# A two-layer decoder trunk on eight cores: the fused stage's turn reordered, decays and gate folded into weights and constants, and loads moved

## The reference

```python
mod = silu(c) @ w_mod[layer] + b_mod[layer]      # 6 rows of 1024
shift_m, scale_m, gate_m, shift_f, scale_f, gate_f = split(mod, 6)
h = rms_norm(x, norm_mix[layer]) * (1 + scale_m) + shift_m
x = x + gate_m * token_mixer(h, ...)
h = rms_norm(x, norm_ffn[layer]) * (1 + scale_f) + shift_f
x = x + gate_f * (swiglu(h) if layer == 0 else moe_swiglu(h))   # top 2 of 8 experts
```

## Time and profile before

| | us |
|---|---|
| median of 3 runs | 4345.12 |
| lowest and highest | 4304.47, 4496.92 |
| the profiled execution | 4326.1 |
| its span, slowest core (1) | 4324.4 |
| spans of the cores | 4235.2 to 4324.4 |
| PE busy | 3081.8 (71%) |
| DVE, ACT, POOL busy | 1214.9, 1066.3, 581.2 |

### The profile page before, as it was taken

The page is one execution under the profiler, slowest core; times in us unless marked ns, Lnnn a source line. Parts: engine busy times, 40 slices in busy tenths (PEclk is TensorE's granted clock), DMA queues, the critical chain, the costliest instruction groups (busy, mean ns, idle before and its releaser), DMA issues.

```text
span 4324.4 us, 48809 instructions; the slowest of 8 cores (4235.2 to 4324.4 us)
## 1 busy us (share of the span) xinstructions
PE 3081.8 (71%) x16488; PEld 1538.1 (36%) x16497; DVE 1214.9 (28%) x1896; ACT 1066.3 (25%) x1873; POOL 581.2 (13%) x644
## 2 busy tenths in 40 slices
PE   2266666676569998788666543999966597768776
PEld 1112222233224444233333222645433254435433
DVE  2223334355512314133443332212111111112111
ACT  2223333333211111355332221212121112112111
POOL 1100000022200101000022221011121121202120
PEclk7566565577789999788677776999988799989998
DMA  5442342301284333313111128649596969698884
GB/s 145 95 116 79 101 116 86 98 25 49 97 122 74 93 59 84 75 24 58 66 39 37 49 64 153 105 70 166 79 164 110 177 102 151 99 150 124 120 132 68
DMA packets 311799, 412.93 MB, mean 95 GB/s; under 512 B 62604, under 2 KB 225956, under 8 KB 311469
## 3 DMA queue, kind: packets, MB, share of 16 engines
q0 software_dynamic: 219056, 257.81, 39.8%
q1 hardware_dynamic: 92414, 150.83, 11.1%
HBM read 577.17 MB, written 59.06 MB: 147 GB/s over the span
## 4 chain that ended last, share of the span: by engine, by line
PE 56%; DMA 17%; DVE 10%; ACT 7%; issue 6%; POOL 1%; SPq 1%; DVEq 0%; ACTq 0%; POOLq 0%; PEldq 0%
PE ps L1430 13%; PE ps L1458 10%; PE ps L1072 7%; DMA t_w2m<-moe_w 5%; DMA t_ring<-moe_w 4%; PE ps L1003 4%; PE ps L1104 4%; PE ps L789 3%; PE ps L754 3%; PE ps L718 3%; DMA t_bm<-b_mod 2%; DMA ebrep<-ebscr 2%; DVE t_mev L613 2%; PE ps L907 2%; DMA t_w<-ffn_w 1%
## 5 line engine op out<-in xcount | busy, mean ns | idle before, releaser
L1430 PE MATMUL ps<-t_hgT,t_ring 128*128 128x0 bf16 (+1 forms) x5376 | 840.0, 318 | 213.1 <-DMA t_ring<-moe_w 109.9
L1430 PEld LDWEIGHTS ps<-t_hgT,t_ring 128*128 128x128 bf16 x5376 | 523.6, 100 | 530.1 <-issue 276.4
L1458 PE MATMUL ps<-t_w2m,t_gTm 128*128 128x512 bf16 x1960 | 434.4, 385 | 81.7 <-DMA t_w2m<-moe_w 80.9
L1434 DVE TENSOR_TENSOR t_gTm<-ps,t_sam 128x384 bf16<-128x384 f32 (+1 forms) x336 | 217.3, 647 | 837.8 <-ACT t_sam L1433 830.6
L1072 PE MATMUL ps<-hT,t_w 128*128 128x512 bf16 x1408 | 311.7, 385 | 41.5 <-DMA t_w<-ffn_w 40.2
L1458 PEld LDWEIGHTS ps<-t_w2m,t_gTm 128*128 128x128 bf16 x1960 | 193.5, 99 | 320.1 <-issue 96.5
L1433 ACT ACTIVATE t_sam<-ps 128x384 bf16<-128x384 f32 (+1 forms) x336 | 187.2, 562 | 473.4 <-PE ps L1430 448.6
L1433 ACT ACT_TABLE_LOAD x56 | 71.8, 1283 | 773.1 <-PE ps L1430 773.1
L754 PE MATMUL ps<-t_qT,t_kT 64*128 64x256 bf16 (+1 forms) x768 | 210.2, 388 | 56.0 <-ACT t_pr L758 50.0
L766 DVE TENSOR_TENSOR t_pr<-t_pr,t_EB 128x512 bf16<-128x512 bf16 (+1 forms) x320 | 127.9, 406 | 415.6 <-ACT t_pr L758 412.4
L907 PE MATMUL ps<-t_wr,hT 128*128 128x512 bf16 x768 | 193.5, 414 | 44.2 <-DVE t_wr L888 44.2
(11 more groups left out here) (241 smaller groups left out, 3090.5 us busy)
## 6 DMA issues: line engine op xcount, KB each, us to landing
t_ring<-moe_w POOLq DMA_DIRECT2D x112, 1024.0 KB, 27.1
t_w2m<-moe_w POOLq DMA_DIRECT2D x56, 1024.0 KB, 38.4
t_wm<-w_mod SPq DMA_DIRECT2D x40, 1024.0 KB, 5.4
t_w<-ffn_w POOLq DMA_DIRECT2D x20, 1024.0 KB, 9.3
t_wmi<-w_mod SPq DMA_DIRECT2D x8, 1024.0 KB, 16.5
t_n0x<-x SPq DMA_DIRECT2D x16, 512.0 KB, 11.3
t_n1x<-x SPq DMA_DIRECT2D x16, 512.0 KB, 3.6
xs<-t_n1x SPq DMA_DIRECT2D x16, 512.0 KB, 2.7
```

Source lines behind the costliest of these rows:

```text
L1430: ins = e.matmul(o, lhsT=ring[:, s_, kc, j * 128:(j + 1) * 128], rhs=r, start=(kc == 0), stop=(kc == 7))
L1434: k.op("dve", lambda e: e.tensor_tensor(out=gT[:, fc, c0:c0 + width], in0=ps[:, bb, 0:width], in1=sa[z][:, 0:width], op=ALU.mult), reads=[ ...
L1458: ins = e.matmul(ps[:, b0 + hf, :], lhsT=gT[:, fc, b * 128:(b + 1) * 128], rhs=w2s[:, fc, hf * 512:(hf + 1) * 512], start=(fc == 0), stop= ...
```

## The change

Constants: the decay of q is no longer multiplied in. It is common to a token's retention output, which the norm per head divides out; only the term 128 EPS under the root is divided by the decay's square (c_dec, added by POOL at L1024 of the new file). The decay of k goes onto v in ACT's copy (four of 128 columns, each with its own scale). The gate of the mixer, gate_m, and the gain ret_gain go into wo (`gated_wo`, on DVE, from fp32 pieces of w_out that SP loads). So the gate product, POOL's product with gB and one DVE pass of the rotary step go.

Order: `eb_rows` stands behind the norm's loop. `proj` alternates between two pairs of banks for the first pair of heads. pv runs three batches behind scores. 12 of the 20 modulation items stay in layer 0, 8 go to layer 1, at fixed batches; all bias rows are loaded once, and DVE adds them. wr, wst, the centring and wo are loaded and worked inside attention. In the fused stage a turn begins with `project`, `evacuate` and `outproj`, and statistics come last. `ffn_open` loads the first two groups of w1 and w3 in turn 16 of layer 0's fused stage, and each group of w2 is loaded one group ahead. Buffers move to make room.

```diff
-    c["c_dec"] = np.concatenate([qdec, kdec], axis=1).astype(np.float32)
+    c["c_dec"] = np.concatenate([128.0 * EPS / qdec ** 2, kdec], axis=1).astype(np.float32)
...
         def residual(self, t, halves, tmpo=None, Btmpo=None):
...
-                for hf, bank in enumerate(halves):
+                for hf, bank in halves:
                     c = slice(512 * hf, 512 * hf + 512)
-                    k.op("dve", lambda e: e.tensor_tensor(out=tmpo[:, c], in0=ps[:, bank, :], in1=gate2[:, g, c], op=ALU.mult),
-                         reads=[PB[bank], GB[g]], writes=[Btmpo])
-            k.op("dve", lambda e: e.tensor_tensor(out=xt, in0=xt, in1=tmpo, op=ALU.add), reads=[Btmpo, Bxt], writes=[Bxt])
+                    k.op("dve", lambda e: e.tensor_tensor(out=xt[:, c], in0=ps[:, bank, :], in1=xt[:, c], op=ALU.add), reads=[PB[bank], Bxt], writes=[Bxt])
...
+    def eb_rows():
         k.dma("sp", bass.AP(ebscr, 0, [[384, 8], [8 * 384, 3], [1, 384]]), ebst[:], reads=[Beb], writes=[ebscr_buf])
-        for i_ in range(24):
+        for i_ in [8 * b_ + h for h in range(8) for b_ in range(3)]:
...
-        k.dma("sp", bm[:], bmod_d[l:l + 1, nb * 512:(nb + 1) * 512], writes=[Bbm])
...
+        k.op("pe", lambda e: e.matmul(ps[0:32, bank, :], lhsT=onesq[:], rhs=mev[:], start=True, stop=True), reads=[Bmev, B["const"]], writes=[PB[bank]])
+        n = len(mod_q)
+        k.op("dve", lambda e: e.tensor_tensor(out=mrow[0:n, :], in0=ps[0:n, bank, :], in1=bm[:], op=ALU.add), reads=[PB[bank], Bbm], writes=[Bmrow])
...
-        for tb in range(4):
-            for j in range(2):
-                r_ = proj(0, j, tb)
-                r_()
+        prev = None
+        for n, (tb, j) in enumerate((tb, j) for tb in range(4) for j in range(2)):
+            rest = proj(0, j, tb, 6 - 2 * (n % 2), 7 - 2 * (n % 2))
+            if prev is not None:
+                prev()
+            prev = rest
+        prev()
...
+        LAG = 3
+        mod_open(12 if l == 0 else 8)
...
-                    if l == 0 and i < 18:
-                        if i % 6 == 2:
-                            mod_half(0)
-                        elif i % 6 == 4:
-                            mod_half(1)
-                        elif i % 6 == 5:
-                            mod_end(7)
+                    if i in (3, 11):
+                        mod_half(0)
+                    elif i in (6, 14):
+                        mod_half(1)
+                    elif i in (8, 16):
+                        mod_end(7)
+                    if (c, hh, i) in late:
+                        late[(c, hh, i)]()
...
+        attention(l, attnT, BattnT, {(1, 0, 1): load_wr, (3, 0, 1): load_late, (3, 0, 9): centre, (3, 1, 1): open_wo, (3, 1, 9): half_wo})
...
+            for h in range(4):
+                c = slice(128 * h, 128 * h + 128)
+                k.op("act", lambda e: e.activation(out=rv[:, t % 5, c], in_=ps[:, 1, c], func=AF.Copy, scale=dec[:, 4 + h:5 + h]), reads=[PB[1], B["oh"]], writes=[Brv[t % 5]])
+            k.op("act", lambda e: e.activation(out=sgg[:, t % 5, :], in_=ps[:, 2, :], func=AF.Silu), reads=[PB[2]], writes=[Bsgg[t % 5]])
...
         for i in range(NT + 9):
+            at(i, 0, project)
+            at(i, 0, evacuate)
+            at(i, 6, outproj)
+            at(i, 4, gated)
+            at(i, 6, lambda t: n2.residual(t, ((1, 4), (0, 7))))
+            at(i, 7, norm_a)
             at(i, 1, turn_qk)
-            at(i, 1, state)
             at(i, 2, inner)
-            at(i, 4, gated)
             at(i, 3, outer)
             at(i, 5, turn_ret)
-            at(i, 6, outproj)
...
+            at(i, 1, state)
             at(i, 8, norm_b)
+            at(i, 6, n2.stats)
...
+    def ffn_open():
+        F["w13"] = P("w13", [128, 2, 2, 8, 512], BF16, 157, n=2)
+        ffn_load13(0)
+        ffn_load13(1)
...
+                if gi + 1 < n:
+                    load2(gi + 1)
```

More of the change, by code:

```diff
@@ L646, in build, with attention @@
         BVg[z_].lo, BVg[z_].hi = vv0 + 24 * KB + 12 * KB * z_, vv0 + 36 * KB + 12 * KB * z_
-    def attention(l, mixT, BmixT):
+    def attention(l, mixT, BmixT, late):
         qT, BqT = P("qT", [128, 2, S], BF16, 48, n=2)
@@ L823, in attention @@
                 pend = None
-                for i in range(nb_ + 2):
+                for i in range(nb_ + LAG):
                     if i < nb_:
@@ L998, in outproj @@
         def outproj(t):
[L999 removed]
+            for hf, bk in ((1, 4), (0, 7)):
                 def mm(e):
@@ L1077, in up @@
                          reads=[PB[bb], Bsa[i2]], writes=[BgT])
-        load13(0)
-        load13(1)
-        for gi in range(n):
-            load2(gi)
+        load2(0)
         n2 = None
```

261 lines of the change are left out of this document (140 added, 121 removed).

## The result

The changed kernel took 3920.7 us in the median of four executions (3867.4 to 4113.4) against 4338.2 for the one before on the same chip; the ratio is 0.898 with a 95% interval of 0.882 to 0.914: faster by about 10%. Two of the four executions ran with one die at a lower clock and are left out of the ratio; the other two took 3867.4 and 3887.6 us. The profiled one is the latter, with a span of 3885.9 us on core 5 (3821.1 to 3885.9 over the cores, clock 0.854 to 0.865; before 4324.4). Forecast for the profiled execution were 3857 us, so 469 of gain; measured are 438.5.

A forecast was written before the change was run, and what follows sets the result against it. The prediction took the fused turns to be bound by a chain, not an engine, with PE waiting on loads elsewhere. Gains of 64+182+8+3+82+40+25+65 = 469 off 4326.1 gave 3857, 3876 us at the median's level, range 3785 to 4000.

The forecast's parts named there:

- Start: Before the first attention: x loads ahead of the 24 table copies, 64 us less, bounds 52 and 74.
- Both attentions: Attention of both layers: modulation items at 3.6 us each instead of 12.7, 182 us less, bounds 134 and 216.
- Entry: Entry of the fused stages: wait for wr goes; 14 and 9 us less, booked as 8 and 3 after DVE's blocks.
- Fused stage, layer 0: Layer 0's fused turns: both PE waits go, 13.2 us a full turn, 82 us less, bounds 45 and 95.
- more is won: Rival for attentions and fused stages: half sums fully covered, clock above 0.85 in both attentions, 3800 us; chance 0.15.
- the clock stays low: Rival for attention and fused stages: PE's clock remains 0.6 to 0.75, about 100 us less gain, 3975 us; chance 0.19.
- FFN: FFN entry, first half's up phase: waits for weights go, 40 us less, bounds 25 and 45.
- Layer 1's own projections: Eight projections before layer 1's attention: 4.1 us each over two bank pairs instead of 7.2, 25 us less.
- Fused stage, layer 1: Layer 1's fused turns: 21 to 24 us, 25.5 with router sum every fourth; 65 us less, bounds 35 and 100.
- Expert stage: From 2590 us to the end: touched nowhere, 1734 us, no gain counted.
- The moves only shift the waits: Rival for SP and POOL queues and DVE's chain: loads arrive as late as before, 4085 us; chance 0.06.
- Slower: Rival in attention: DVE half sums waiting for w_mod block PE over 11.7 us each; 4475 us at 15 each; chance 0.02.

The follow-up runs named there:

- tables first: Changed kernel with the table copies put back ahead of the last eight x loads: attention's products start at 269.8 us, against 222.4 in the changed kernel.
- the run with the bias rows alone: Kernel before, with only the bias rows loaded at once and added on DVE: span 4199.7 us, ratio 0.973 to the kernel before.
- Spreading the steps: Changed kernel with an item's eight DVE steps issued one per attention batch, not in two blocks of four: timed runs 3806 and 3808 us.
- The old order in the changed kernel: Changed kernel with a fused turn's steps back in the earlier order, folds of gate and decay kept: layer 0 turns 16.7 us, span 95 us longer.
- Four pairs: Changed kernel with four PSUM bank pairs for attention's own projections, a buffer per table copy and six copies ahead of wv: attention's products start at 165.8 us.
- the experiment on layer 1's turn: Changed kernel with q and k copied ahead of ACT's cast and lo right behind the cast: layer 1's fused stage 355.0 us, 39.6 less.
- combined kernel: Changed kernel with weights apart, six tables first, four bank pairs, sums spread, layer 1's turn and banks, and blocks late: 3628.0 us profiled, ratio 0.842 to before.

## Why the prediction was right, and where it was not

The forecast of 3876 us (3785 to 4000) held, 45 us under the median: the mechanisms named were those at work, and 438.5 of 469 us came. But that the sum came so near is partly luck: it hides larger errors of opposite sign. The attentions, the start, the entry and layer 1's own projections gave some 72 us less than forecast, the fused stages with the drain some 44 more. (The bounds, too, were added up loosely: as listed they give 4034 and 3765, not 3990 to 4030 and 3775. The range given holds either way.)

*Start, 64 forecast, 58.7 measured.* The queues behaved as worked out: copies to 187 (183), V's last load asked for by 219 (landed 219), EB and wqk at 222 (215). The old place of the copies costs 47 us (tables first). The forecast called the quicker projections hidden in this, and in the changed kernel they are: PE is through them 28 us early. They show, with 11 us, only where the tables come first.

*Both attentions, 170 forecast (182 less 12 for DVE's blocks), 121.1 measured, at the lower bound of 122.* This is the term that was mis-sized. "I take 3.6 us an item" assumed that pv three batches behind scores covers the first half sum and leaves little of the second. The item costs 1.9 of product and 2.94 of wait, so 4.8, and about 1 us that no row names. The check "under 1.5 us before each modulation sum" failed with 2.94. In the run with the bias rows alone, pv stood only two batches behind, and the wait was 2.2 us an item; nothing shows that the third batch covers anything. Spreading the steps showed the cause: with the wait gone, the two attentions fall by 74.8 us. The other part is DVE's blocks (centring, w_out), priced at 6 us a layer: spread, they give 7.3 and 10.6. Taking these 17.9 for them and 293.5 for plain attention twice, it is (720.5 - 587.0 - 17.9)/20 = 5.8 us an item, just under the bound of 6. So of the 49 us that are missing, 44 are the items (2.2 us each) and 6 the blocks. With the sums spread it is (645.7 - 587.0 - 17.9)/20 = 2.0, near the other bound of 1.9, though part of that is other products running faster.

*Entry, 14 forecast in layer 0, 7.9 measured.* The first rope step comes 8.1 us after attention's last DVE step (7.6 forecast; before it was 20.8, and the prediction's 21.4 counts from that step's start), so 12.6 us came as far as there. The rest went in the new order itself: the first rqk transposes now stand behind the second projection, for which PE waits 6.4 us.

*Fused stage, layer 0, 82 forecast, 95 in the turns and 15 in the drain.* A full turn took 12.1 us, not 13.2, as PE's clock went to 1.00 and not part of the way: PE busy falls to 10.9 us a turn, 90% of it. That is the "more is won" rival's number in this stage, while attention went the way of "the clock stays low". ACT's four copies of v take 1.73 us in place of 0.59 (1.1 to 1.6 forecast, and 1.0 by the prediction's other estimate), and no wait of PE in these turns is for them. The drain was forecast to give nothing on balance; POOL's stand for weights was there (17.0 us, 23 forecast) and reached PE with 16.5 (14), but the rest of the drain won some 31 us and not 14; why is not shown. The old order in the changed kernel says that the reason was right but told only half: the prediction gave both waits to the order, and the rqk wait goes with the folds alone (3.80 to 0.63 us), so that 3.8 of the 8.4 us a turn stay without the new order.

*FFN, 40 forecast for both its places.* 1.3 us of waits are left of the 41.5 of the earlier trace rows; the two up phases take 155.6 and 154.3 us. Right.

*Layer 1's own projections, 25 forecast, 12.9 measured.* "4.1 each": they took 5.6. With two pairs of banks, a projection still waits 2.5 to 2.8 us (once 4.1) for DVE to empty the bank of the one before last. Four pairs bring them to 2.5 each (19.8 for all eight), and the stretch to 50.5.

*Fused stage, layer 1, 74 forecast with its entry, 90.1 measured.* The new wait behind the cast and the wait on lo were both there as written, 4.5 and 3.8 us. The turn of 23.5 us on average (164.2/7) was put at 25.5. Both waits going gave 39.6 us, as the experiment on layer 1's turn shows.

*Expert stage.* Unchanged (1740 against 1736), as counted.

*The rivals.* "The clock stays low" was true for attention (0.69 and 0.72, an item at 5.8 us), false for layer 0's fused stage; layer 1's stayed at 0.77 and was still quicker than forecast. "The moves only shift the waits" was false as a whole, but the table copies show its pattern: what moved was again at the end of a chain, with PE waiting 28 us. "Slower" needs a half sum blocked for 11.7 us by its load; DVE waited for w_mod once in the changed kernel's attentions, 3.1 us. It waited long only in experiments: 30 and 35 us where 18 copies and V's loads stood in front of w_mod, and 18 us where the spread steps ask for it from the first batch on.

## What to carry to other kernels

When a long wait is removed, price what it hid: look for the next operand of the same instruction and ask how long its producer occupies its in-order engine in one block; eight short steps between the work of others cost PE 0.4 us ahead of twelve products here, and the same steps in two blocks 35.4, of which not all was won, since a part came back at other products. When steps are reordered and passes removed at once, put back each by itself before calling either the cause: here one of the two waits was gone without the new order. Copies that wait for one another are slow by themselves, but let loose they slow the load that PE needs next: ask first for what is used first, and put the rest behind the load that comes next, w_mod here, and not ahead of it (that last step was not run).

## What the runs showed that was not expected

- The granted clock rose over a whole stage once its waits were short: 1.00 through filling and full turns of layer 0's fused stage, where it had been 0.86 and 0.75. Over full turns of layer 0 it was 0.75 with 7.0 us of waits in a turn of 20.5 (before), 0.86 with 4.1 in 16.7 (old order) and 1.00 with 1.2 in 12.1; over those of layer 1 it was 0.77, 0.84 and 0.92 in the changed kernel and the two that take its waits away. The fp32 product of the sums fell from 1046 to 699 ns on the mean (649 in the combined kernel's second attention) when only a wait in front of it was removed. The Trainium skill (TensorE: Matmul & The Clock Gate, section "HAM oscillation — how this bites in real kernels") has short bursts between waits begin slow every time; the traces agree, with 1046 ns for the product behind a wait and 699 without. Removing 58.8 us of waits ahead of the products gave 74.8, of which 27.2 are PE's own time.
- Let loose, 24 copies of 192 KB kept SP for 26.7 us instead of 96.0, and the load of wv beside them took twice as long to reach PE (28 us against 14, and 8.5 with six copies ahead of it).
- The expert stage differs by up to 42 us from run to run (1706 to 1748) with no edit to it, more than several of the effects looked for; only stages cut at events could be compared to a few microseconds.
